# DeltaNet inverse on TensorE: the second direction crosses the array's halves, and attention stores its heads one by one

## What is computed

```python
lower = jnp.where(strict, jnp.einsum('bhnid,bhnjd->bhnij', k_beta, k) * decay, 0.0)
rhs = jnp.concatenate([v * beta[..., None], k_beta * jnp.exp(gc)[..., None]], axis=-1)
sol = lax.linalg.triangular_solve(jnp.eye(C, dtype=f32) + lower, rhs,
                                  left_side=True, lower=True, unit_diagonal=True)
u, w = sol[..., :dv], sol[..., dv:]
```

## Time and profile before

| | us |
|---|---|
| median of 3 runs (3658.97 to 3667.17) | 3659.43 |
| the profiled execution's own time | 3664.0 |
| its span | 3662.2 |
| PE busy in the span | 3383.6 (92%) |
| DVE, ACT, POOL busy | 1096.1, 880.6, 508.5 |
| DeltaNet prepare of layer 0, from the phase's first instruction to the scan's first | 524.9 to 715.1 |
| DeltaNet prepare of layer 1, the same | 2390.9 to about 2579 |

### The profile page before, as it was taken

How to read it: one execution, slowest core, us unless ns; L and a number is a source line. 1 busy time by engine, 2 the same in 40 slices (tenths; PEclk the granted TensorE clock), 3 DMA queues, 4 the chain that set the end, 5 groups by cost and what they waited for, 6 DMA issues and landing times. The chain is left out here.

```text
span 3662.2 us, 59952 instructions
## 1 busy us (share of the span) xinstructions
PE 3383.6 (92%) x22912; PEld 1934.2 (53%) x22913; DVE 1096.1 (30%) x2588; ACT 880.6 (24%) x1770; POOL 508.5 (14%) x568
## 2 busy tenths in 40 slices
PE   6998979989899999999986998989898999999996
PEld 3555659855444444444432645769644444444442
DVE  2424534445311111111125435434442111111114
ACT  2223432232211111111122223422221111111112
POOL 0100014120100000000033010042210000000004
PEclk8998989999999999999997999989899999999998
DMA  9702310123378886978877103100335899999965
GB/s 354 287 9 103 135 66 4 61 96 137 129 300 329 326 353 227 363 294 329 328 269 273 50 20 117 70 17 4 131 155 195 344 363 363 360 363 363 362 248 218
DMA packets 137842, 779.71 MB, mean 213 GB/s; under 512 B 12976, under 2 KB 33328, under 8 KB 100912
## 3 DMA queue, kind: packets, MB, share of 16 engines
q1 hardware_dynamic: 79184, 564.07, 39.4%
q0 software_dynamic: 33120, 120.60, 9.3%
q10 hardware_dynamic: 25344, 92.29, 6.2%
HBM read 640.59 MB, written 136.31 MB: 212 GB/s over the span
## 5 line engine op out<-in xcount | busy, mean ns | idle before, releaser
L2176 PE MATMUL psum<-arena 128*128 x2336 | 1039.1, 596 | 15.7 <-issue 15.7
L2176 PEld LDWEIGHTS psum<-arena 128*128 128x128 f32 x2336 | 432.5, 190 | 558.5 <-issue 558.5
L2187 PE MATMUL psum<-arena 128*128 x1168 | 515.3, 593 | 0.0
L760 PE MATMUL psum<-arena 128*128 128x480 f32 (+3 forms) x1088 | 398.0, 521 | 3.2 <-ACT arena L592 3.2
L2157 POOL DMA_INDIRECT arena<-h,arena x146 | 137.6, 943 | 1530.2 <-PE psum L2170 1505.3
L2187 PEld LDWEIGHTS psum<-arena 128*128 128x128 f32 x1168 | 214.6, 189 | 245.8 <-issue 245.8
L2237 ACT ACTIVATE arena<-psum 128x256 f32<-128x256 f32 x146 | 56.2, 385 | 1033.8 <-PE psum L2176 1033.8
L760 PEld LDWEIGHTS psum<-arena 128*128 128x128 f32 x1088 | 204.6, 191 | 176.6 <-issue 165.7
L2281 DVE COPY arena<-psum 128x512 f32<-128x512 f32 x146 | 101.1, 692 | 421.8 <-PE psum L2187 421.8
L2272 DVE COPY arena<-psum 128x256 f32<-128x256 f32 x73 | 31.0, 425 | 520.9 <-PE psum L2182 520.9
L2270 DVE TENSOR_TENSOR arena<-arena,psum 128x256 f32<-128x256 f32 x73 | 30.8, 422 | 488.3 <-ACT arena L2237 488.3
(11 more groups left out here) (338 smaller groups left out, 3811.6 us busy)
## 6 DMA issues: line engine op xcount, KB each, us to landing
arena<-in_w_gu SPq DMA_DIRECT2D x130, 2048.0 KB, 8.7
arena<-in_w_dn SPq DMA_DIRECT2D x130, 1024.0 KB, 12.1
y_slots<-arena ACTq DMA_DIRECT2D x156, 512.0 KB, 9.4
arena<-in_ada SPq DMA_DIRECT2D x24, 2048.0 KB, 7.7
y_slots<-arena SPq DMA_DIRECT2D x8, 4096.0 KB, 32.9
arena<-in_w_gdn SPq DMA_DIRECT2D x6, 1536.0 KB, 15.8
arena<-in_w_out SPq DMA_DIRECT2D x2, 4096.0 KB, 14.4
arena<-in_w_tok SPq DMA_DIRECT2D x4, 1920.0 KB, 8.0
```

Of the source, the lines that this page charges most:

```text
L760: last = nc.tensor.matmul(bank(n, wide), lhsT[:, k], rhs[:, k], start=(k == 0), stop=(k == DK - 1))
L2176: last = nc.tensor.matmul(psum[:, 2 + r, :], xT[:, r, k * P:(k + 1) * P], W[:, bass.ds(slot + k * 2 * DE, 2 * DE)], start=(k == 0), stop=( ...
L2187: last = nc.tensor.matmul(psum[:, (LEFT, RIGHT)[n][r], :], hT[:, r, j * P:(j + 1) * P], W[:, bass.ds(slot + DK * 2 * DE + j * D + n * 512, ...
```

## The change

In `attention`, SP waits for each head's last unit and stores that head's 64 columns by itself: ten DMAs in place of two, the last of them after the last unit.

In `prepare`, direction 1 keeps `X` and `DT` with the two chunks in swapped halves of the partitions (`other(d, r)`). `lower` and `turn_inverse` of direction 1 then go from one half of the rows to the other half of the columns, the two quarters that direction 0 leaves free, and their loops alternate both directions head by head behind the waits of both. `correct` is as before. POOL's first level of direction 1 crosses the halves, with two multiplications of 64 partitions in place of one of 128. At the end `move_back` (12 products on PE) and `take_moved` (a copy on ACT) bring direction 1's `DT` back to the normal halves in a new tile `DN`, which `solve` reads for direction 1.

```diff
-                        sp.wait_ge(out_done, NU)
-                        for a, b in ((0, SWA_H * HD), ((SWA_H + GH) * HD, D)):
-                            sp.dma_start(cat_dram[0:nq * P, a:b].rearrange("(i p) n -> p i n", p=P), cat[:, :, a:b]).then_inc(cat_out, 16)
-                        sp.wait_ge(cat_out, 32)
+                        for h in range(SWA_H + MH):
+                            sp.wait_ge(out_done, (h + 1) * nq)
+                            a = h * HD if h < SWA_H else (SWA_H + GH + h - SWA_H) * HD
+                            sp.dma_start(cat_dram[0:nq * P, a:a + HD].rearrange("(i p) n -> p i n", p=P), cat[:, :, a:a + HD]).then_inc(cat_out, 16)
+                        sp.wait_ge(cat_out, 16 * (SWA_H + MH))
...
+                other = lambda d, r: half(r if d == 0 else 1 - r)
+                DTN = lambda G, d: DT[:, G % 3, 0] if d == 0 else DN[:, G % 2]
...
+                        def take_moved(G):
+                            act.wait_ge(moved, G + 1)
+                            nc.scalar.copy(DN[:, G % 2], psum[:, 4 + chain(G, 1), 0:GW]).then_inc(move_copied, 1)
...
                             if a == 2 and G:
+                                take_moved(G - 1)
                                 tail(G - 1)
...
-                                nc.gpsimd.tensor_tensor(v6(DT[:, H % 3, d]), v6(WT[:, H, d]), b6(cst("level", lo, lo + CHUNK)), ALU.mult).then_inc(masked, 1)
-                                pool.wait_ge(masked, n + 1)
+                                if d == 0:
+                                    nc.gpsimd.tensor_tensor(v6(DT[:, H % 3, d]), v6(WT[:, H, d]), b6(cst("level", lo, lo + CHUNK)), ALU.mult).then_inc(masked, 1)
+                                    pool.wait_ge(masked, 3 * H + 1)
+                                else:
+                                    pool.wait_ge(dt1_done, 2 * H + 1)
+                                    for r in range(2):
+                                        level = cst("level", lo, lo + CHUNK)[half(r)].unsqueeze(1).to_broadcast([CHUNK, GH, CHUNK])
+                                        nc.gpsimd.tensor_tensor(v6(DT[other(d, r), H % 3, d]), v6(WT[half(r), H, d]), level, ALU.mult).then_inc(masked, 1)
+                                        pool.wait_ge(masked, 3 * H + 2 + r)
...
                         def lower(G, v):
                             for d in range(2):
-                                c = chain(G, d)
-                                pe.wait_ge(d_done[c], nth(G, v - 1) + 1)
-                                for m, q in heads:
+                                pe.wait_ge(d_done[chain(G, d)], nth(G, v - 1) + 1)
+                            for m, q in heads:
+                                b = blk(q, m)
+                                for d in range(2):
+                                    c = chain(G, d)
                                     for r in range(2):
-                                        b = blk(q, m)
-                                        last = nc.tensor.matmul(psum[half(r), 4 + c, b], WT[half(r), G, d, b], U[half(r), G, d, b], start=True, stop=True)
-                                last.then_inc(x_prod[c], 1)
+                                        last = nc.tensor.matmul(psum[other(d, r), 4 + c, b], WT[half(r), G, d, b], U[half(r), G, d, b], start=True, stop=True)
+                                    if (m, q) == heads[-1]:
+                                        last.then_inc(x_prod[c], 1)
...
                                     for r in range(2):
-                                        b = blk(q, m)
-                                        last = nc.tensor.matmul(psum[half(r), 4 + c, b], DT[half(r), G % 3, d, b], cst("unit")[half(r)], start=True, stop=True)
-                                last.then_inc(tr_done[c], 1)
+                                        last = nc.tensor.matmul(psum[half(r), 4 + c, b], DT[other(d, r), G % 3, d, b], cst("unit")[other(d, r)], start=True, stop=True)
+                                    if (m, q) == heads[-1]:
+                                        last.then_inc(tr_done[c], 1)
+
+                        def move_back(G):
+                            c = chain(G, 1)
+                            pe.wait_ge(dt_done[c], nth(G, LAST - 1) + 1)
+                            for m, q in heads:
+                                for r in range(2):
+                                    b = blk(q, m)
+                                    last = nc.tensor.matmul(psum[half(r), 4 + c, b], cst("unit")[other(1, r)], DT[other(1, r), G % 3, 1, b], start=True, stop=True)
+                            last.then_inc(moved, 1)
...
                             for d in range(2):
                                 c = chain(G, d)
-                                pe.wait_ge(dt_done[c], nth(G, LAST - 1) + 1)
+                                if d == 0:
+                                    pe.wait_ge(dt_done[c], nth(G, LAST - 1) + 1)
+                                else:
+                                    pe.wait_ge(move_copied, G + 1)
...
+                            if a == 2 and G:
+                                move_back(G - 1)
                             for T, v in live:
                                 lower(T, v)
```

More of the change, by code:

```diff
@@ L1074, in phase_gdn_prepare @@
                 DT = sbuf(st, "DT", [P, 3, 2, GW])
+                DN = sbuf(st, "DN", [P, 2, GW])
                 kg = sbuf(st, "kg", [P, 2, 2, GW])
@@ L1088, in phase_gdn_prepare @@
                     S("q_turned"), S("q_copied"), S("ko_done"), S("kg_done"))
+                moved, move_copied = S("moved"), S("move_copied")
                 masked, dt1_done, u_prod, wt_prod, u_copied, wt_copied = (
@@ L1308, in solve @@
                                     for r in range(2):
-                                        last = nc.tensor.matmul(psum[half(r), 4 + c, h * HD:(h + 1) * HD], DT[half(r), G % 3, d, blk(q, m)],
+                                        last = nc.tensor.matmul(psum[half(r), 4 + c, h * HD:(h + 1) * HD], DTN(G, d)[half(r), blk(q, m)],
                                                                 feat[half(r), G, (2 * GH + h) * HD:(2 * GH + h + 1) * HD], start=True, stop=True)
@@ L1316, in solve @@
                                         last = nc.tensor.matmul(psum[half(q), 2 + r, 192 * d + m * HD:192 * d + (m + 1) * HD],
-                                                                kg[half(r), G % 2, d, h * HD:(h + 1) * HD], DT[half(r), G % 3, d, blk(q, m)], start=True, stop=True)
+                                                                kg[half(r), G % 2, d, h * HD:(h + 1) * HD], DTN(G, d)[half(r), blk(q, m)], start=True, stop=True)
                                 last.then_inc(wt_prod, 1)
```

3 lines of the change are left out of this document (1 added, 2 removed).

## The result

The changed kernel takes 3671.73 us (median, 3667.15 to 3681.55) against 3664.46 for the kernel before in the same comparison: ratio 1.0027, 95% interval 1.0015 to 1.0039. I had forecast 3631 us. A second comparison gave 1.0038 (1.0025 to 1.0052). So it is slower by about 0.3%, where 0.8% less was expected.

The account below looks back on a forecast made before the run. PE was taken to bound prepare's full periods, a DMA the end of attention. Prepare -22 us for two layers and stores -6 gave -28 from 3659.43, so 3631.4 us; bounds 3616 to 3645, range drawn 3614 to 3650.

Parts of the forecast that it names:

- The four-quarter rate, 16.9 ns: PE's `lower` and `turn_inverse` in prepare: 16.9 ns per instruction on four quarters against 29.2 on two; bounds 14.6 to 19.2.
- A one-tile slot, 5.93 us: Prepare where one tile alone is live: a slot grows from 4.64 to 5.93 us, 1.3 more.
- The phase's start: Start of prepare: +0.9 us per layer from `exponents` queued behind POOL's added work, and +1.1 for G = 0.
- The stores: End of attention: the next phase starts earlier, 6 us less over both layers, bounds 4.6 and 7.6.
- A full period, -3.4 us: Prepare, G = 1 to 4: -5.9 PE work, +0.7 `move_back`, +1.8 waits; 28.05 us falls to about 24.6.
- From the fourth period to the end of the phase: End of prepare: -3.4 us for the fourth full period, -1.1 for G = 5, +2.7 for G = 6.
- Rival 1: Prepare's 96-instruction groups lose the four-quarter rate as instructions must be supplied; at 25 ns slower, 3678 us; 8 in 100.
- Rival 4, the clock,: PE's clock falls in prepare's one-tile stretches where it waits more; 3671 us; 1 in 100, counted within the supply rival.

Follow-up runs that it names:

- stores-alone kernel: The kernel before with only the stores by head, prepare unchanged; ratio 0.9974 (0.9965 to 0.9983).
- `lower` twice: The changed kernel with each matmul of `lower` issued twice in a row, same results and waits; timed once, 3753 us.
- directions apart: The changed kernel with `lower` and `turn_inverse` one direction after the other, each behind its own wait, on the new quarters; ratio 0.9991 (0.9982 to 1.0001).
- the last form: The kernel before with stores by head, full-array transposes in `turn_inverse`, `WT` regrouped on POOL, four-quarter `lower` behind each direction's own wait; ratio 0.9898, median 3625 us.

## Why the prediction was wrong

- *The four-quarter rate, 16.9 ns:* held, and more: 15.1 ns over 96 matmuls by the same measure, near the lower bound of 14.6. By that rate the forecast would have promised more still.
- *A one-tile slot, 5.93 us:* right. Timeline of the changed kernel, `lower` to `lower` 700.61 to 706.50, 5.89 us, with the waits where the text had them:

```profile
700.61 0.93 PE L1293 MATMUL psum<-arena 64*64 64x64 f32 x48 [1.03 <-ACT arena L1147]
...
702.18 1.61 PE L1304 MATMUL psum<-arena 64*64 64x64 f32 x48 [0.64 <-DVE arena L1412]
...
704.54 0.93 PE L1320 MATMUL psum<-arena 64*64 64x64 f32 x48 [0.75 <-DVE arena L1418]
```

- *The phase's start:* first instruction to the second tile's gate rows 45.5 us against 43.9 in layer 0 and 44.4 against 41.8 in layer 1, +1.6 and +2.6; forecast +0.9 and +1.1, together 2.0. Near, but the clock differs: in 534 to 552 us it was granted 0.69 before and 0.90 after. The stores-alone kernel, with the old prepare and 0.99 there, took 41.9.
- *The stores:* 7.5 us in the traces, 6 forecast, at the upper bound of 7.6. The last store of 192 KB landed after 2.3 us in the stores-alone kernel, where 2.5 was taken.
- ***A full period, -3.4 us:* the step that failed.** Three of them gave -1.4 us together (565.14 to 647.64 against 568.77 to 652.70) where -10.3 was expected. The sum took PE's work and the waits between engines, and no third resource. A four-quarter group uses up 66 pairs a microsecond (15.1 ns each) where 33 come. At 3.85 us per 128 the 903 pairs of a period are 27.2 us, and the periods measured are 27.1 to 28.2. That figure is the mean of the same trace and so no test by itself; the tests are `lower` twice, which moved the period as supply had it, and the packets, behind which the gaps end. The kernel before, at 879 pairs and 28.0 us, was 6% away from this count, and the change took array time off it and put instructions on.
- *From the fourth period to the end of the phase:* +5.1 where -1.8 was forecast (-3.4 - 1.1 + 2.7). With the directions apart, on the same quarters and with the same instructions, it is +1.2. So 3.9 of the 5.1 us are the lock, that is the waits of both directions with the interleaving: the waits, 1.3 us more in a one-tile slot, came as forecast, but the shorter groups that were to pay for them in the periods with two tiles didn't shorten them.
- *Rival 1* named the supply at which instructions must come, but priced it as a slower group (25 ns) and argued against it from a group of 48. The rate of a group was never the question; what counts is the mean over 128 pairs, 30.1 ns. The direction was the rival's, the chance of 8 in 100 too small, since its own condition ("the instructions must be supplied at that pace") had been answered with a row that could not test it. The hint was in the trace of before: 21 packets in 84 us, and a gap marked issue within a group at 701 us:

```profile
701.12 0.50 PE L1283 MATMUL psum<-arena 64*64 64x64 f32 x10 [0.16 <-issue]
```

- *Rival 4, the clock,* was set aside with "the granted clock stayed 1.00". In the first trace it stayed so from 552 to 712 us, and it fell to 0.74, 0.92 and 0.93 in windows of two others. That the rival's price, 3671 us, is the measured median is chance: in the profiled execution, 3667 us, prepare lost nothing to the clock there. How much of the loss it holds in the median was not measured.

What stays open: why a block takes 3.85 us. It isn't the transfer itself. A packet of 16 KB takes 1.09 us on the mean (1.7% of 16 engines' 84 us, over 21 packets), and in no trace do two of them overlap: at least 2.27 us lie between the end of one and the start of the next. The 1.0 to 1.7 us until the next packet starts, its own 0.9 to 1.5 and the 1.2 to 1.5 until TensorE goes on make up the 3.3 to 3.9 us. No run changed any of the three.

## What to carry to other kernels

Before making small matmuls faster, count them: divide the instructions of a stretch by its time and compare with the densest stretch that any trace of the kernel sustains over several hundred instructions; a short fast group shows nothing about supply. Where that limit is near, take instructions away first (three full-array transposes in place of 24 small matmul instructions) and make the engine faster afterwards. A lock between two independent chains is not needed to make them overlap on different quarters of the array: neighbouring groups did it in part by themselves, and without the lock the last form gained 23 us more (3648 to 3625).

## What the hardware showed that I had not expected

- TensorE's 64x64 float32 matmuls were supplied at 33.0 to 33.2 a microsecond over the same 84 us of three kernels, in blocks of 256 instructions, one in 3.85 us on the mean, though they did different work; the densest 84 us named above have 34.5 a microsecond. Over a single block 3.55 us occurred. The packet itself took 1.09 us, and no two overlapped.
- Groups of 24 matmuls on two quarters each, one after the other on different quarters, ran at 22 ns a matmul against 29.2 on the same quarters and 15.1 interleaved.
- PSUM copies of 64x192 on ACT went one every 0.34 us (16 in 5.41) where one of 128x384 took 0.48: four small ones cost 2.8 times one large.
- A store of 192 KB in pieces of 256 bytes landed after 3.4 us in the median, beside attention's work, and after 2.3 alone.
